# Moving the attention parts' view of the activations from 192 to 64 bytes past the start of their tile

## The reference

```python
qkv = x @ w_qkv                      # first block, layer 2
q, k, v = jnp.split(qkv, 3, axis=-1)
...
x = _layernorm(ALPHA * x + _swiglu(x, w_gate[i], w_up[i], w_down[i]), ln_ffn_g[i], ln_ffn_b[i])
...
proj = xn @ w_in                     # second block
(qa, ka, va, qb, kb, vb, qi, ki, wi, xc, yc, gates) = jnp.split(proj, IN_OFFSETS, axis=-1)
...
g = jax.nn.sigmoid(gates).reshape(B, S, N_BRANCHES, D_MODEL)
merged = g[:, :, 0] * (y_a @ w_pa) + g[:, :, 1] * (y_b @ w_pb) + g[:, :, 2] * (y_c @ w_pc)
return merged @ w_o
```

## Time and profile before

| | |
|---|---|
| median of the runs | 951.16 us |
| span of the profiled execution | 949.5 us |
| the profiled execution's own time, span and what lies around it | not listed apart; the median is 1.7 us above the span |
| PE busy | 938.3 us, 99% |
| VectorE busy | 668.8 us, 70% |
| ScalarE busy | 473.1 us, 50% |
| mean bandwidth of the DMAs | 185 GB/s |

### The profile page before, as it was taken

One profiled execution on the slowest core, in us unless ns is written; L12 is line 12 of the kernel. 1 busy time (PEld: TensorE's weight loads), 2 busy tenths in 40 slices (PEclk: granted clock), 3 DMA queues, 4 the chain that ended last, 5 costly groups with the idle time before them and its releaser, 6 DMA issues.

```text
span 949.5 us, 15378 instructions
## 1 busy us (share of the span) xinstructions
PE 938.3 (99%) x5895; PEld 830.4 (87%) x5895; DVE 668.8 (70%) x964; ACT 473.1 (50%) x730; POOL 34.6 (4%) x63
## 2 busy tenths in 40 slices
PE   9999999999999999999999999999999999999997
PEld 7988888888898988888887889899999888888886
DVE  4876767676787886667668587975976676666663
ACT  4544444435666454443445566568664454434432
POOL 2010001000000001000001000000000000000000
PEclk9999999999999999999999999999999999999999
DMA  8686666539533377665653945444665546655531
GB/s 295 202 284 227 199 219 209 204 133 266 147 130 101 117 249 256 213 207 178 206 182 109 265 137 134 136 134 137 219 217 181 193 142 213 203 181 189 208 135 44
DMA packets 141648, 175.67 MB, mean 185 GB/s; under 512 B 7152, under 2 KB 119985, under 8 KB 141598
## 3 DMA queue, kind: packets, MB, share of 16 engines
q1 hardware_dynamic: 138384, 166.55, 54.5%
q0 software_dynamic: 2656, 8.31, 2.5%
q10 hardware_dynamic: 558, 0.12, 0.1%
HBM read 173.88 MB, written 1.09 MB: 184 GB/s over the span
## 4 chain that ended last, share of the span: by engine, by line
PE 93%; DVE 5%; issue 1%; ACT 1%; POOL 0%; DVEq 0%; POOLq 0%
PE bank L506 91%; DVE w_lo L1149 1%; PE bank L844 1%; PE bank L638 1%; DVE x_rows L1573 1%; DVE x_rows L1580 1%; DVE stats L1565 1%; ACT w_hi L1137 0%; DVE x_both L1552 0%; DVE arena L2011 0%; PE bank L650 0%; ACT arena L1310 0%; DVE arena L1824 0%; PE bank L717 0%; DVE vareps L1541 0%
## 5 line engine op out<-in xcount | busy, mean ns | idle before, releaser
L1149 DVE TENSOR_TENSOR w_lo<-raw,w_hi 128x1024 fp32r<-128x1024 f32 x308 | 362.6, 1220 | 87.3 <-ACT w_hi L1137 86.8
L506 PE MATMUL bank<-x_both,w_hi 128*128 128x256 f32 (+2 forms) x2032 | 408.3, 325 | 0.0
L506 PEld LDWEIGHTS bank<-x_both,w_hi 128*128 128x128 f32 (+1 forms) x2032 | 336.7, 188 | 37.0 <-issue 5.5
L1137 ACT ACTIVATE w_hi<-raw 128x1024 fp32r<-128x1024 f32 x308 | 307.9, 1050 | 98.1 <-PE bank L506 93.6
L506 PE MATMUL bank<-x_both,w_lo 128*128 128x256 f32 (+1 forms) x1432 | 272.4, 281 | 0.0
L506 PEld LDWEIGHTS bank<-x_both,w_lo 128*128 128x128 f32 (+1 forms) x1432 | 217.0, 190 | 2.6
L506 PE MATMUL bank<-w_hi,arena_r 128*128 128x512 f32 x672 | 189.6, 391 | 0.2 <-DVE arena_r L1712 0.2
L506 PEld LDWEIGHTS bank<-w_hi,arena_r 128*128 128x128 f32 x672 | 124.6, 188 | 25.6 <-issue 0.8
L506 PE MATMUL bank<-w_lo,arena_r 128*128 128x512 f32 x336 | 106.2, 389 | 0.0
L1628 DVE TENSOR_REDUCE arena<-bank 128x512 f32<-128x1024 f32 x52 | 63.5, 1222 | 47.9 <-PE bank L506 47.9
L506 PE MATMUL bank<-w_hi,x_both 128*128 128x512 f32 (+1 forms) x352 | 75.8, 346 | 0.6 <-ACT w_hi L1137 0.4
(11 more groups left out here) (179 smaller groups left out, 604.3 us busy)
## 6 DMA issues: line engine op xcount, KB each, us to landing
raw<-w_up SPq DMA_DIRECT2D x76, 512.0 KB, 4.5
raw<-w_down SPq DMA_DIRECT2D x76, 512.0 KB, 4.2
raw<-w_in SPq DMA_DIRECT2D x60, 512.0 KB, 4.6
raw<-w_gate SPq DMA_DIRECT2D x44, 512.0 KB, 4.7
raw<-w_qkv SPq DMA_DIRECT2D x24, 512.0 KB, 4.8
raw<-w_o SPq DMA_DIRECT2D x16, 512.0 KB, 4.3
table<-bias_vectors POOLq DMA_DIRECT2D x12, 256.0 KB, 4.8
raw<-w_pa SPq DMA_DIRECT2D x4, 512.0 KB, 4.4
```

The costliest lines, as they stand in the source:

```text
L506: return nc.tensor.matmul(*a, skip_group_check=True, **k)
L1137: nc.scalar.activation(w_hi[slot][:, c], raw[slot][:, c], ACT.Copy).then_inc(hi_done, 1)
L1149: last = nc.vector.tensor_tensor(w_lo[slot][:, c], raw[slot][:, c], w_hi[slot][:, c].bitcast(F32), ALU.subtract)
```

## The change

The shifted view starts 16 floats (64 bytes) into the tile in place of 48 (192 bytes). The tile keeps its size, so that no tensor behind it moves, and `arena_r`, which uses `SHIFT` too, keeps its views. `x_far` now starts at 192 modulo 256 bytes. The built programs hold the same instructions in the same order with the same waits. 1,864 of them have another address: 1,848 matmuls that read the view, 8 ACTIVATEs of ScalarE and 8 TENSOR_TENSORs of VectorE that write it.

```diff
 V_NORM, O_NORM, MIX_NORM = 1, 2, 4
 SHIFT = 48
+FAR = 16
 KI_COLS = DH + IDX_HEADS
...
         x_cells = sb("x_both", [P, KT * 2 * SEQ + SHIFT], F32R)
-        x_both, x_far = (x_cells[:, at:at + KT * 2 * SEQ].rearrange("p (k t) -> p k t", k=KT) for at in (0, SHIFT))
+        x_both, x_far = (x_cells[:, at:at + KT * 2 * SEQ].rearrange("p (k t) -> p k t", k=KT) for at in (0, FAR))
```

## The result

The changed kernel takes 956.42 us (median of five, 956.04 to 956.71) against 951.16 us: 0.55% slower, ratio 1.0055 with a 95% interval of 1.0045 to 1.0066. That is +5.3 us where +8.5 was forecast, inside the range, in the forecast direction, and 3.3 us short of the forecast. The 958.4 to 964.0 us that the likeliest case gave by itself were missed by 2 us. The spans of the two profiled executions differ by 954.9 - 949.5 = 5.4 us.

What follows compares the result with a forecast made beforehand. TensorE's matmul pace was taken to bound the kernel. Fast units +7.8, slow units +1.0, keys +0.1 and view-stationary matmuls -0.4 made +8.5 us on 951.2, giving 959.7 us; range 949.3 to 964.5.

Steps and rivals of the forecast that it cites:

- the likeliest case: Slower through distance 64: moving-view matmuls at 120.0 ns, +8.5 us in all, 959.7 us, by itself 958.4 to 964.0; chance 0.58.
- The bound: Five stretches reading the shifted view: TensorE busy 319.6 of 323.3 us, so matmul pace reaches the program's end almost one for one.
- Distance as the key: Matmuls: moving operand's start address less the stationary one's, modulo 256 bytes, orders the paces; 1,656 go 192 to 64, 192 the reverse.
- The strict reading of the two independent ports: TensorE's SBUF reads: operands' relative placement would not matter, sum zero, 951.2 us; chance counted within the no-change 0.22.
- The price of distance 64 with 256 columns: Matmuls with the shifted view moving: taken as 120.0 ns, between 113.3 and 122.2; 25 fast units +7.8 us.
- my second rival: Projection units: distance 64 leaves only the slow pace, all at 117.7 ns, +5.0 less 0.4 us, 955.8 us; chance 0.08.
- the slow ones: 9 projection units already at 117.7 ns: 432 matmuls go to 120.0 ns, +1.0 us.
- the keys: Indexer keys: 24 matmuls with the shifted view moving, at 117.5 ns, each lose 2.5 ns, +0.1 us.
- The 192 matmuls with the view stationary: V rows, first and second values, 512 columns: go from distance 64 to 192 at 226.7 ns, -0.4 us (-1.7 to +0.4).
- A period of 128 bytes: Address matters only within 128 bytes, so moving matmuls keep 113.5 and 117.7 ns: 951.2 us, -1.8 to +1.9; no-change chance 0.22.
- all units turn fast: Projection units: none falls into the slow pace at distance 64, -2.3 to -3.6 us, about 948.3 us; chance 0.12.

## Why the prediction was right, and where its sizes were off

**The bound.** Right. PE's pace went to the end one for one: 5.4 us of span for 5.7 us more of busy time, PE's idle time in the five stretches did not grow, the granted clock stayed at 1.00, and the writes to `x_both` take 690 ns at the median on VectorE, as before (691).

**Distance as the key.** Right, and shown by the run that moved the weights: the paces went with the distance, not with the remainder of the activations' own address. Distance alone does not fix a pace, though, since 64, 160 and 192 each have two. The strict reading of the two independent ports in the Trainium skill ("TensorE: Matmul & The Clock Gate", "Step-by-step: what each phase is for") would have given no change. The same instruction at 113.3, 117.7 and 119.8 ns by the other operand's address decides against that reading.

**The price of distance 64 with 256 columns.** The step that was off, and the largest term of the sum. I took 120.0 from the row at distance 0 because the 512-column row at 64 was worse than at 0. It measured 117.7, which is what my second rival gave; its sum, 955.8, is nearer to 956.42 than my 959.7. The two forms don't order the distances alike: with 256 columns 192 is the best and 0 the worst, with 512 columns 0 is the best, and 192 is the worst of those that I knew or used (233.3, shared by 32 and 96). An argument from one form to the other has no force here. The gates grew by 2.7 us, not 3.9. With 117.7 in place of 120.0 the terms read 24 x 48 x 4.2 = +4.8 us (24 units lost the fast pace, one did not) and nothing for the slow ones and the keys (24 in 2.82 us before and after).

**The 192 matmuls with the view stationary.** Wrong in sign. I took -0.4 us from bounds of -1.7 and +0.4. They rose from 228.9 to 233.3: 192 x 4.4 = +0.8 us, above the upper bound. The lower bound had carried the gain of the 256-column form over to them, the same mistake. Together +5.6 us, against 5.4 in the spans.

**Where luck came in.** The case that I gave 0.58, all units at 120.0, did not come. What came is the pace of the case that I gave 0.08, all but one unit at 117.7. The time lies in the stated range because that range reached down to no change, 949.3 us, and not because the likeliest case was right in size.

**The rivals.** A period of 128 bytes is refuted. That all units turn fast did not come; the two paces at one distance, on which that rival and the slow-pace one rested, are real, and an extra call ahead of a unit can switch between them.

What stays open is which relation of the reads makes a pace steady. Also open is what sets the pace of a unit at its start. That the two operands are read at once and get in each other's way is a guess that no run contradicts and none shows, and neither pairing that I tried explains the kernels in which high and low parts lie apart. With 256 columns seven distances were run; 144, 208 and 240 bytes and most below 128 were not, so a better place than 192 is not excluded.

## What to carry to other kernels

Where TensorE is the bound, as here, try the start addresses of its two operands relative to each other, modulo 256 bytes. In this kernel they were worth up to 5.6% of the pace (113.3 against 120.0 ns with 256 columns) and 2.8% with 512 (226.7 against 233.3). Measure it for each form at the addresses themselves: places 16 bytes apart differed by 6 ns here. Both kernels in which the distance changed from matmul to matmul were over 9 us slower than the one before, so keep the matmuls of a unit at one distance. Compare the pace from start to start, unit by unit, since one distance can hold two steady paces.

## What the runs showed of the hardware that was not expected

- Two steady paces at one distance, 113.3 and 117.7 ns, held from the fourth or a slightly later matmul of a unit to its end, and changed in some units by an extra call of 128 columns ahead of them.
- 16 bytes are enough: 113.3 ns at distance 192, 119.3 at 176.
- With 512 columns distances 32, 96 and 192 all give 233.3 ns, 6.6 above distance 0.
- The Trainium skill, "TensorE: Matmul & The Clock Gate", section "Back-to-back issue gap", gives N / 2.4 + 2.5 ns for what it calls the isolated gap between warm matmuls, which an estimate turns into 109.2 ns with 256 columns and 215.8 with 512, and about 131 ns a matmul as measured for a sustained stream of 512 columns. The traces agree with neither: no projection ran faster than 113.3 ns and no 512-column stream faster than 226.7, so an estimate by the formula would be 4% to 9% short for this kernel's forms.
